# One encoder layer in fp32: the sum into v ahead of late weight rows, pair 0's scores first, decayed keys on ScalarE, output-weight sums on VectorE, one gate ahead of one normalisation

## The chip, the core and the metric

The kernel runs on one core of a Trainium2 chip. The metric is the device time of one execution in microseconds (us), and a time is the median of several runs.

The engines are called as the profile calls them. PE is TensorE (PEld its weight loads), DVE is VectorE, ACT is ScalarE, POOL is GpSimd. SP is SyncE, which only issues transfers (its queue is SPq).

## The reference

The program computes one encoder layer for two sequences of 1024 tokens with 1024 channels. Cut to what matters here:

```
h = rmsnorm(x) * (1 + scale1) + shift1                  # scale, shift, gate: silu(c) @ w_ada + b_ada
q, k, v, g_sw, p, gate_a, gate_b = split(h @ w_in)      # 8 heads, dk = 64, dv = 128
q, k = rope(q), rope(k) / 8
per chunk of 128 tokens, forward and backward:
    inner = ((q_c @ k_c.T) * decay_in) @ v_c
    cross = (q_c * decay_q) @ state
    state = decay_chunk * state + (k_c * decay_k).T @ v_c
ret      = forward + backward, normalised per head
branch_a = silu(g_sw) * ret * gain
branch_b = (pooled(p) @ w_pool) * pool_scale
merged   = sigmoid(gate_a) * branch_a + sigmoid(gate_b) * branch_b
x = x + gate1 * (merged @ w_out)
x = x + gate2 * mlp(modulated rmsnorm(x))               # up, 3-tap convolution, gelu * linear, down
y = rmsnorm(x)
```

## The kernel before

**Precision and products.** Every large product is made of passes over a high and a low fp32r part of the operands. ACT copies a raw weight piece to its high part, POOL subtracts to get the low part. Products of 2 x 2 blocks are done with 7 block products instead of 8. For that, sums of weight quarters are needed (POOL makes most of them) and sums of results (DVE adds a PSUM bank into a tile that ACT has copied).

**Stages.** For each sequence: the mixer in four head pairs (`pr` 0 to 3, two heads each), the output product (`out`), the norm of the middle, the MLP. This change touches the mixer's four pairs and what the output product reads.

**Order.** Each engine runs its own list, written out by hand, and waits on counting semaphores. Nothing is reordered at run time, so an instruction that waits holds up all that stands behind it on its engine, and this is as true of SP's list of transfers.

**One pair on PE.** In pairs 1 to 3: seven qkv products (o = 0 to 6, `qkv_products`, L1457). The last of them, o = 6, adds into a bank whose other half must first have been added to v, so it waits for `q_summed` 2, which DVE's `qkv_add(1)` (L2810, v_sb) gives. Then `pool_unit` (L1476) with the turning of q and k between its halves, the scores (L1555), and 21 unit products (L1525), written (s, o) with s = 0 to 2 and o = 0 to 6. Behind certain of these stand the small products: `products(h)`, keys times values (KV0, KV1; L1544), which waits for DVE's `scores(h)` (L2879) and for the decayed keys (`kd_done`); `outputs(h)` (O0, O1; L1569); `turn_ret(h)` (TR0, TR1; L1310), which waits for DVE's `normed(h)` (L2910); and `branch_b(h)` (BB0, BB1; L1579). Unit product (1, 6) waits for DVE's `unit_add(1, 1)` (L2819, bufA). Pair 0 makes q, k and v in another way (`first_qkv`) and has the scores behind (0, 3), KV0 behind (0, 4).

**DVE in a pair.** Besides these it makes four levels of the pooling (`pool_level`, L2985), the recurrent states (L2866), the statistics, the swish and the gates. All of it is one list per pair, printed below.

**Late rows.** 32 tiles of 128 x 1024 of w_ada per sequence (`late_tile`, L2647) are reduced on DVE in spots 0 to 5 of each pair, two in a spot, as `LATE_AT` says: none ahead of spot 4 of pair 0, none after spot 1 of pair 3. They sit in a ring of two buffers. SP loads one (L773) when the tile two before it has been reduced, at a fixed place among the other loads.

**Sums of output weights.** For the output product of both sequences, four units u of w_out (each 128 x 4 x 512, 1 MB) are loaded into `out_unit` (L890), summed in place by four subtractions or additions, and stored to DRAM (`out_sums`, L895). There is one buffer, so load u + 1 waits for store u, which waits for sums u. Its memory is that of the late rows' ring, so load 0 waits for the last late tile. All this lies in sequence 0, pair 3, and before this change the sums run on POOL, between weight pieces.

## Time and profile before

| | |
|---|---|
| median of 3 runs | 2626.63 us (2625.64 to 2629.75) |
| the profiled execution's own time | 2632.94 us |
| its span, first to last instruction | 2631.1 us |
| mean granted clock of PE | 0.984 |
| busy: PE, DVE, POOL, ACT | 2536.4, 1866.0, 1732.4, 1145.4 us |

The span is read from the first instruction to the last; the execution's own time is 1.8 us longer. The profiled execution lies 6.3 us above the median of the runs. Sequence 0's mixer pairs take 96 to 600 us of the span, sequence 1's 1394 to 1888 us. In a timeline row the first number is the start, the second the time that the merged instructions take together, and the bracket behind it says how long the engine had stood still before them and who released it.

### The profile page before, as it was taken

The numbers are of one execution on the slowest core, as the hardware profiler recorded it, in microseconds if no ns is written. First come the engines' busy times: TensorE is split into PE (matmuls) and PEld (weight loads), VectorE is DVE, ScalarE is ACT, GpSimd is POOL, SyncE is SP. The second block draws the span as 40 slices with busy tenths as digits, with TensorE's granted clock in tenths as the row PEclk, the third lists the DMA queues.
The fourth block names the chain that finished last, engine by engine and source line by source line (L and its number), as shares of the span: only waits on it lengthen the run. The fifth ranks groups of instructions, "written<-read, shape, count | busy, mean of one in ns | idle before, by whom it ended". The sixth has DMA issues, their size and how long they took to land.

```text
span 2631.1 us, 34797 instructions
## 1 busy us (share of the span) xinstructions
PE 2536.4 (96%) x12684; PEld 2121.1 (81%) x12684; DVE 1866.0 (71%) x2246; ACT 1145.4 (44%) x1738; POOL 1732.4 (66%) x1181
## 2 busy tenths in 40 slices
PE   6899999989999999999998999999999999999998
PEld 3788888868778888878887888888877888888886
DVE  4978898866786666665868888888778645556434
ACT  5332323225555454555623323232456545454443
POOL 1675767786287777645656858586564877775545
PEclk9999999999999999999999999999999999999998
DMA  8124242346144455497631423332440333325764
GB/s 325 40 83 133 82 133 83 110 175 221 48 147 138 160 172 169 153 322 249 190 114 41 131 84 110 105 111 73 167 149 25 112 112 112 110 80 185 213 194 145
DMA packets 296010, 362.15 MB, mean 138 GB/s; under 512 B 17313, under 2 KB 178465, under 8 KB 295841
## 3 DMA queue, kind: packets, MB, share of 16 engines
q1 hardware_dynamic: 292960, 349.44, 41.2%
q10 hardware_dynamic: 2880, 10.49, 1.1%
q8 instruction: 103, 1.69, 0.3%
q14 instruction: 67, 0.54, 0.1%
HBM read 284.36 MB, written 75.50 MB: 137 GB/s over the span
## 4 chain that ended last, share of the span: by engine, by line
PE 65%; DVE 15%; POOL 7%; issue 6%; DMA 4%; ACT 3%; SPq 1%; DVEq 0%; POOLq 0%; ACTq 0%
PE ps L1095 26%; PE ps L1261 14%; PE ps L1525 7%; PE ps L1156 4%; PE ps L1476 3%; POOL f_w L2162 3%; PE ps L1366 2%; PE ps L1457 2%; DVE late_rows L2647 2%; PE ps L1193 2%; DMA late_rows<-in_w_late 2%; PE ps L1544 1%; DVE merged_t L2962 1%; POOL grs L2183 1%; DVE bufB L2924 1%
## 5 line engine op out<-in xcount | busy, mean ns | idle before, releaser
L2223 POOL TENSOR_TENSOR f_w<-f_ring,f_w 128x512 fp32r<-128x512 f32 x434 | 596.1, 1379 | 399.3 <-ACT f_w L1812 394.0
L1095 PE MATMUL ps<-hc_hi,f_w 128*128 128x512 f32 x2240 | 690.5, 389 | 3.5 <-ACT u_act L1886 2.8
L2162 POOL TENSOR_TENSOR f_w<-f_ring,f_w 128x512 fp32r<-128x512 f32 x282 | 443.7, 1585 | 301.8 <-ACT f_w L1646 301.7
L1095 PEld LDWEIGHTS ps<-hc_hi,f_w 128*128 128x128 f32 x2240 | 419.9, 188 | 93.1 <-ACT u_act L1886 3.6
L1095 PE MATMUL ps<-hc_lo,f_w 128*128 128x512 f32 x1120 | 435.8, 389 | 0.0
L1261 PE MATMUL ps<-act_ring,f_w 128*128 128x512 f32 x1848 | 421.7, 390 | 3.8 <-DVE act_ring L2542 2.9
L1261 PEld LDWEIGHTS ps<-act_ring,f_w 128*128 128x128 f32 x1848 | 346.5, 188 | 77.9 <-issue 4.9
L1812 ACT ACTIVATE f_w<-f_ring 128x512 fp32r<-128x512 f32 x434 | 269.8, 624 | 256.3 <-POOL f_ring L2233 109.5
L1525 PE MATMUL ps<-hb,f_w 128*128 128x512 f32 x1440 | 349.2, 397 | 2.7 <-POOL f_w L2162 2.2
L1646 ACT ACTIVATE f_w<-f_ring 128x512 fp32r<-128x512 f32 x282 | 175.4, 627 | 369.6 <-POOL f_ring L2170 140.2
L1525 PEld LDWEIGHTS ps<-hb,f_w 128*128 128x128 f32 x1440 | 268.8, 189 | 65.4 <-issue 9.6
L2542 DVE TENSOR_TENSOR act_ring<-f_ring,act_ring 128x512 fp32r<-128x512 f32 x154 | 149.8, 978 | 173.2 <-ACT act_ring L1864 172.8
L1095 PEld LDWEIGHTS ps<-hc_lo,f_w 128*128 128x128 f32 x1120 | 210.2, 188 | 43.7
L1457 PE MATMUL ps<-f_w,hb 128*128 128x256 f32 x1440 | 174.7, 283 | 0.0
L1457 PEld LDWEIGHTS ps<-f_w,hb 128*128 128x128 f32 x1440 | 174.0, 192 | 0.5
L1864 ACT ACTIVATE act_ring<-f_ring 128x512 fp32r<-128x512 f32 x154 | 97.0, 630 | 162.7 <-PE ps L1261 147.7
L1156 PE MATMUL ps<-out_ring,f_w 128*128 128x512 f32 x672 | 154.7, 391 | 0.2 <-DVE xT L2563 0.2
L1525 PE MATMUL ps<-ht,f_w 128*128 128x512 f32 x576 | 144.2, 400 | 8.0 <-ACT gate_rows L1682 7.3
L1156 PEld LDWEIGHTS ps<-out_ring,f_w 128*128 128x128 f32 x672 | 125.9, 188 | 27.6 <-issue 1.0
L1525 PEld LDWEIGHTS ps<-ht,f_w 128*128 128x128 f32 x576 | 107.0, 190 | 32.8 <-ACT gate_rows L1682 8.9
L2647 DVE SCALAR_TENSOR_TENSOR late_rows<-late_rows,silu_row 128x1024 f32<-128x1024 f32 x64 | 108.9, 1736 | 26.5 <-DMA late_rows<-in_w_late 26.5
L2249 POOL TENSOR_TENSOR f_w<-f_ring,f_w 128x512 fp32r<-128x512 f32 x56 | 82.7, 1484 | 50.5 <-ACT f_w L1829 50.1
(263 smaller groups left out, 4109.5 us busy)
## 6 DMA issues: line engine op xcount, KB each, us to landing
f_ring<-in_w_in SPq DMA_DIRECT2D x176, 256.0 KB, 4.9
f_ring<-in_w_up SPq DMA_DIRECT2D x160, 256.0 KB, 3.3
f_ring<-gated_out SPq DMA_DIRECT2D x154, 256.0 KB, 3.0
late_rows<-in_w_late SPq DMA_DIRECT2D x64, 512.0 KB, 3.7
gated_out<-gated_up SPq DMA_DIRECT2D x44, 512.0 KB, 4.2
f_ring<-down_sums SPq DMA_DIRECT2D x88, 256.0 KB, 3.0
gated_out<-t_gated SPq DMA_DIRECT2D x22, 768.0 KB, 6.5
f_ring<-in_w_down SPq DMA_DIRECT2D x66, 256.0 KB, 3.5
```

Of the source, the lines that this page charges most:

```text
L1095: ins = pe.matmul(ps_row[:, half_of(bank)], a[:, cols], b, start=i in (0, 1, 3) and k == 0 and n == 0, stop=k == KQ - 1 and n == 2, skip_g ...
L1156: ins = pe.matmul(ps_row[:, half_of(bank)], a[:, j * P:(j + 1) * P], b, start=i in (0, 1, 3) and c == 0 and o == 0, stop=c == PAIRS - 1 an ...
L1261: ins = pe.matmul(ps_row[:, half_of(bank)], a[:, j * P:(j + 1) * P], b, start=i in (0, 1, 3) and c == 0 and p == 0, stop=c == CHUNK_PAIRS ...
L1457: ins = pe.matmul(ps[:, Q_SLOT[i], t * 2 * P:(t + 1) * 2 * P], a[:, k, rows], b[:, cols], start=i in (0, 1, 3) and k == 0 and n == 0 and t ...
L1525: ins = pe.matmul(ps_row[:, half_of(bank)], a[:, cols], b, start=i in (0, 1, 3) and k == 0 and n == 0, stop=k == KQ - 1 and n == 2, skip_g ...
L1646: act.activation(mix_out(pr, q)[:, 0, :], mix_raw(mix_load(pr, q)), ACT.Copy).then_inc(mix_hi.sem, 1)
L1812: act.activation(piece_slot(q)[:, 0, :], piece_raw(q), ACT.Copy).then_inc(piece_hi.sem, 1)
L1864: act.activation(act_of(where[1], m)[0], ring_slot(UP_LOADS + 2 * m + 1), ACT.Copy).then_inc(a_hi.sem, 1)
L2162: pool.tensor_tensor(out[:, 1, :], raw, out[:, 0, :].bitcast(F32), ALU.subtract).then_inc(mix_lo.sem, 1)
L2223: pool.tensor_tensor(piece_slot(q)[:, 1, :], piece_raw(q), piece_slot(q)[:, 0, :].bitcast(F32), ALU.subtract).then_inc(piece_lo.sem, 1)
L2542: dve.tensor_tensor(low, ring_slot(UP_LOADS + 2 * m + 1), high.bitcast(F32), ALU.subtract).then_inc(a_lo.sem, 1)
L2647: dve.scalar_tensor_tensor(rows, rows, 0.5, silu_row[seq][:, :], ALU.mult, ALU.mult, accum_out=modT[:, seq, 16 + n:17 + n]).then_inc(late_ ...
```

## The change

Five things are moved. (1) In pairs 1 to 3, `qkv_add(1)`, the sum into v, comes ahead of the two late tiles of spot 1. SP issues the late loads of spot 5 two loads earlier. (2) In pair 0, DVE does the pooling levels and `scores(0)` ahead of `decayed_q(0)`, `unit_add(0, 2)` and `pool_means` behind the first states, and `swish(1)` right behind `swish(0)`; O1 stands behind (1, 5) instead of (1, 4). (3) `decayed_k(h)`, two multiplications of 128 x 8 x 64 for each head, goes from DVE to ACT, in every pair. (4) The four sums of each output unit go from POOL to DVE, at spots 2 to 5 of pair 3, and SP's loads and stores of the units are spread accordingly. (5) `gate_a(1)` comes ahead of `normed(1)`, in every pair.

```diff
-OUT_UNIT_AT = (("set", 0, 3), ("set", 1, 0), ("set", 1, 4), ("set", 2, 1))
+OUT_UNIT_AT = (2, 3, 4, 5)
...
-                    for j in range(KC - 2):
+                    for j in range(KC - 4):
                         mix_in(where, j)
                     late_loads(pr - 1, 5)
-                    for j in range(KC - 2, KC):
+                    for j in range(KC - 4, KC):
                         mix_in(where, j)
...
                     if with_units:
-                        for u in range(1, PAIRS - 1):
-                            out_unit_store(u)
-                            out_unit_load(u + 1)
+                        out_unit_store(1)
+                        out_unit_load(2)
...
                 for j in range(4):
                     out_ring_load(out, j)
+                if seq == 0:
+                    out_unit_store(2)
+                    out_unit_load(3)
                 sp.wait_ge(*filled(last_pair, "TR1"))
...
+            def decayed_k(where, h):
+
+                kdp, scale = mix_buffers[where[1]][2], T_DK + 2 * h
+                if h:
+                    act.wait_ge(*filled(where, "TK"))
+                else:
+                    act.wait_ge(*rope_done.at(where, 2 if where[2] else 4))
...
+                    ins = act.activation(dst, rot[:, :, P + h * DK:P + (h + 1) * DK], ACT.Copy,
+                                         scale=pairS[:, scale + d:scale + d + 1])
...
                     if pr:
                         copy_p(pair, 0)
+                        decayed_k(pair, 0)
                     piece_after(pair, p_piece(pr, 0))
                     if pr:
                         evac_k(pair)
+                        decayed_k(pair, 1)
                     else:
                         t_piece_high(pair, 3)
                     copy_p(pair, 1)
+                    if pr == 0:
+                        decayed_k(pair, 0)
...
+            def out_unit_sums(u):
+
+                a11, a12, a21, a22 = (out_unit[:, x, :] for x in range(4))
+                dve.wait_ge(unit_in, 32 * (u + 1))
...
                     def late(spot):
 
+                        if seq == 0 and pr == PAIRS - 1 and spot in OUT_UNIT_AT:
+                            out_unit_sums(OUT_UNIT_AT.index(spot))
...
                         late(0)
                         qkv_add(0)
                         rope_half(0)
+                        qkv_add(1)
                         late(1)
-                        qkv_add(1)
                         qkv_add(2)
...
+                    gate_a(1)
                     normed(1)
-                    gate_a(1)
```

DVE's list in sequence 0, pair 0, from the last low part of h (hb) to the second `scores`, before (rot is `scores(0)`, kdp from ps is `scores(1)`):

```order
L2760 TENSOR_TENSOR hb<-xT_49,hb 128x2048
L2833 TENSOR_SCALAR kdp_56<-rot,pairS 128x8x64 x2
L2985 SCALAR_TENSOR_TENSOR poolU<-p_in,pairS 128x1039
L3003 COPY qT_58<-ps 128x1024
L2833 TENSOR_SCALAR rot<-rot,pairS 128x8x64 x2
L2847 TENSOR_TENSOR qdT_59<-qT_58,dec 64x1024 x2
L2985 SCALAR_TENSOR_TENSOR poolU<-poolU,pairS 128x1037
L2985 SCALAR_TENSOR_TENSOR poolU<-poolU,pairS 128x1033
L2819 TENSOR_TENSOR swish_60<-swish_60,ps 128x512
L2879 SCALAR_TENSOR_TENSOR rot<-ps,dec 128x8x128
```

The same place in the changed kernel:

```order
L2785 TENSOR_TENSOR hb<-xT_49,hb 128x2048
L2993 SCALAR_TENSOR_TENSOR poolU<-p_in,pairS 128x1039
L3011 COPY qT_58<-ps 128x1024
L2993 SCALAR_TENSOR_TENSOR poolU<-poolU,pairS 128x1037
L2993 SCALAR_TENSOR_TENSOR poolU<-poolU,pairS 128x1033
L2993 SCALAR_TENSOR_TENSOR poolU<-poolU,pairS 128x1025
L2887 SCALAR_TENSOR_TENSOR rot<-ps,dec 128x8x128
L2844 TENSOR_TENSOR swish_60<-swish_60,ps 128x512
L2844 TENSOR_TENSOR bufB<-bufB,ps 128x512
L2855 TENSOR_TENSOR qdT_59<-qT_58,dec 64x1024 x2
L2887 SCALAR_TENSOR_TENSOR kdp_56<-ps,dec 128x1024
```

The decayed keys are gone from DVE, and `decayed_q` has gone from ahead of `scores(0)` to behind it.

DVE's list in a later pair, around the sum into v (v_sb), before:

```order
L2802 TENSOR_TENSOR rot<-bufA,bufB 128x16x32
L2647 SCALAR_TENSOR_TENSOR late_rows_0_74,modT<-late_rows_0_74,silu_row_72 128x1024
L2647 SCALAR_TENSOR_TENSOR late_rows_1_75,modT<-late_rows_1_75,silu_row_72 128x1024
L2810 TENSOR_TENSOR v_sb<-v_sb,ps 128x1024
L2810 TENSOR_TENSOR rot<-rot,ps 128x1024
```

And in the changed kernel:

```order
L2827 TENSOR_TENSOR rot<-bufA,bufB 128x16x32
L2835 TENSOR_TENSOR v_sb<-v_sb,ps 128x1024
L2670 SCALAR_TENSOR_TENSOR late_rows_0_74,modT<-late_rows_0_74,silu_row_72 128x1024
L2670 SCALAR_TENSOR_TENSOR late_rows_1_75,modT<-late_rows_1_75,silu_row_72 128x1024
L2835 TENSOR_TENSOR rot<-rot,ps 128x1024
```

The sum into v stands two late tiles earlier.

SP's list of transfers in sequence 0, pair 3, from load 0 of the units on, before (xT rows are x coming back, f_ring from w_out or merged_out are the first loads of the output product):

```order
L890 DMA out_unit<-in_w_out 128x2x512 x2
L802 DMA f_ring<-in_w_in 128x4x128 x4
L895 DMA out_sums<-out_unit 128x4x512
L890 DMA out_unit<-in_w_out 128x2x512 x2
L895 DMA out_sums<-out_unit 128x4x512
L890 DMA out_unit<-in_w_out 128x2x512 x2
L895 DMA out_sums<-out_unit 128x4x512
L890 DMA out_unit<-in_w_out 128x2x512 x2
L945 DMA xT_49<-in_xt 128x1024 x4
```

In the changed kernel:

```order
L890 DMA out_unit<-in_w_out 128x2x512 x2
L802 DMA f_ring<-in_w_in 128x4x128 x4
L895 DMA out_sums<-out_unit 128x4x512
L890 DMA out_unit<-in_w_out 128x2x512 x2
L945 DMA xT_49<-in_xt 128x1024 x4
L924 DMA f_ring<-in_w_out 128x512
L924 DMA f_ring<-merged_out 128x512
L924 DMA f_ring<-in_w_out 128x512
L924 DMA f_ring<-merged_out 128x512
L895 DMA out_sums<-out_unit 128x4x512
L890 DMA out_unit<-in_w_out 128x2x512 x2
```

The last piece starts at load 1 (load 0 and store 0 stand before it, with two f_ring loads between them). Load 3 now stands behind the four xT loads and the first four loads of the output product, where before all four unit loads stood ahead of them.

## Rows read from the trace of the kernel before

**Rows 1.** Part 1 of the page: busy time, share, instructions.

```profile
PE 2536.4 (96%) x12684; PEld 2121.1 (81%) x12684; DVE 1866.0 (71%) x2246; ACT 1145.4 (44%) x1738; POOL 1732.4 (66%) x1181
```

**Rows 2.** PE's waits over the whole span: total, times, longest, in us.

```profile
PE ps L1457 <- DVE v_sb L2810: 22.0, 6, 4.5
...
PE ps L1544 <- DVE rot L2879: 13.1, 2, 6.7
```

**Rows 3.** PE's waits in sequence 1's mixer alone, 1380 to 1890 us.

```profile
PE ps L1525 <- ACT gate_rows L1682: 2.3, 2, 1.7
```

**Rows 4.** PE's timeline: o = 5 of pair 1, first and last of six o = 6.

```profile
214.18 5.92 PE L1457 MATMUL ps<-f_w,hb 128*128 128x256 f32 x48
224.61 8.22 PE L1457 MATMUL ps<-f_w,ht 128*128 128x256 f32 x48 [4.51 <-DVE v_sb L2810]
...
1792.38 7.52 PE L1457 MATMUL ps<-f_w,ht 128*128 128x256 f32 x48 [2.79 <-DVE v_sb L2810]
```

**Rows 5.** Stretch of o = 6 in pair 1: length, PE busy, granted clock, DMA.

```profile
224.60:232.70 8.10, 8.09 (x49) 0.69 0.51 166
```

**Rows 6.** DVE's timeline around the sum into v, sequence 0, pair 1.

```profile
220.00 1.21 DVE L2647 SCALAR_TENSOR_TENSOR late_rows<-late_rows,silu_row 128x1024 f32<-128x1024 f32 x1
...
223.35 1.21 DVE L2810 TENSOR_TENSOR v_sb<-v_sb,ps 128x1024 f32<-128x1024 f32 x1
```

**Rows 7.** DVE's timeline at spot 5 of pair 0.

```profile
183.69 1.68 DVE L2647 SCALAR_TENSOR_TENSOR late_rows<-late_rows,silu_row 128x1024 f32<-128x1024 f32 x1 [4.62 <-DMA late_rows<-in_w_late]
```

**Rows 8.** PE's timeline in pair 0: KV0, KV1, and (1, 6).

```profile
120.60 3.58 PE L1544 MATMUL ps<-v_sb,kdp 128*128 128x128 f32 x16 [6.65 <-DVE rot L2879]
...
129.48 1.95 PE L1544 MATMUL ps<-v_sb,rot 128*128 128x128 f32 x16
...
156.37 2.89 PE L1525 MATMUL ps<-ht,f_w 128*128 128x512 f32 x12
```

**Rows 9.** DVE's timeline in pair 0: from decayed keys to unit_add(1, 1).

```profile
101.71 2.94 DVE L2833 TENSOR_SCALAR kdp<-rot,pairS 128x512 f32<-128x512 f32 x2
...
109.78 4.52 DVE L2847 TENSOR_TENSOR qdT<-qT,dec 64x1024 f32<-64x1024 f32 x2
114.33 4.40 DVE L2985 SCALAR_TENSOR_TENSOR poolU<-poolU,pairS 128x1037 f32<-128x1037 f32 x2
...
119.24 1.21 DVE L2879 SCALAR_TENSOR_TENSOR rot<-ps,dec 128x1024 f32<-128x1024 f32 x1
...
138.46 0.17 DVE L2854 MEMSET state<- 64x128 f32 x1 [2.74 <-PE ps L1570]
...
154.49 0.68 DVE L2819 TENSOR_TENSOR bufA<-bufA,ps 128x512 f32<-128x512 f32 x1
```

**Rows 10.** ACT's copies of 128 x 512, line L1682: ns min/median/max, starts.

```profile
L1682 ACT ACTIVATE swish<-ps x16: 596/597/598, 101.9 to 1824.8; 128x512 f32<-128x512 f32 x16
```

**Rows 11.** DVE's sums of the MLP's weight units, line L2536: ns min/median/max.

```profile
L2536 DVE TENSOR_TENSOR down_unit<-down_unit x44: 679/954/1783, 761.8 to 1152.3; 128x512 f32<-128x512 f32 x44
```

**Rows 12.** Loads of the output units, line L890.

```profile
DMA to landing us min/median/max: 3.7/4.8/5.5
```

**Rows 13.** Stores of the output units, line L895.

```profile
DMA to landing us min/median/max: 4.3/4.9/5.7
```

**Rows 14.** PE's timeline: o = 6 of pair 3 and start of out, both sequences.

```profile
492.53 7.48 PE L1457 MATMUL ps<-f_w,ht 128*128 128x256 f32 x48 [2.89 <-DVE v_sb L2810]
...
599.90 23.96 PE L1156 MATMUL ps<-out_ring,f_w 128*128 128x512 f32 x105
...
1877.02 1.03 PE L1310 MATMUL ps<-cst,tokb 128*128 128x128 f32 x8
...
1887.84 12.40 PE L1156 MATMUL ps<-out_ring,f_w 128*128 128x512 f32 x54
```

**Rows 15.** DVE's timeline, sequence 1, pair 3: `normed(0)` and the end of `branch_a(0)`.

```profile
1854.62 2.21 DVE L2910 TENSOR_TENSOR tokb<-tokb,grs 128x1024 f32<-128x1024 f32 x1
...
1866.74 1.27 DVE L2933 SCALAR_TENSOR_TENSOR swish<-ps,pairS,swish 128x1024 f32<-128x1024 f32 x1
```

More of the change, by code:

```diff
@@ L999, in _ @@
                     late_loads(pr, 2)
-                    for j in range(KC + 8, KC + 10):
-                        mix_in(where, j)
                     if with_units:
@@ L1004, in _ @@
                         out_unit_load(0)
+                    for j in range(KC + 8, KC + 10):
+                        mix_in(where, j)
                     late_loads(pr, 3)
-                    for j in range(KC + 10, MIX_LOADS):
-                        mix_in(where, j)
                     if with_units:
@@ L3040, in _ @@
                         states(0)
+                        unit_add(0, 2)
+                        pool_means()
                     else:
```

67 lines of the change are left out of this document (27 added, 40 removed).

## The prediction

> **What bounds the kernel now.** I read the busy times first. PE is busy 96% of the span, all others 71% or less [rows 1], so time can only be won where PE stands still or runs slowly, and every microsecond that it waits is one of the program, so long as PE is not merely made to wait at the next place. The second view is PE's waits. Outside the start, two groups stand out: six waits for the sum into v, 22.0 us, and two for `scores(0)` in pair 0, 13.1 us [rows 2]. A third, for ACT's copies in the gate sets, is 2.3 us in sequence 1's pair 0 [rows 3]; sequence 0's pair 0 is built alike, which makes 4.6. The third view is the timeline behind a wait. The 48 matmuls of o = 5 take 5.92 us, the same 48 of o = 6 behind the wait take 8.22 us in the first case and 7.52 in the last [rows 4]. In that stretch the granted clock is 0.69 of full: part of it runs at 1.2 GHz instead of 2.4 [rows 5]. So a wait of 2.8 us or more costs 1.6 to 2.3 us on top. The excess at the six places is between 6 x 1.6 and 6 x 2.3; most are near the low end, I take 10.8, which is their sum over the six rows. KV0 in pair 0 shows the same: 3.58 us against 1.95 for KV1 [rows 8], 1.6 more, twice.
>
> **The sum into v.** PE has finished o = 5 at 220.1 and waits until 224.6 [rows 4]. DVE meanwhile reduces two late tiles, from 220.0 to 223.4, and only then adds, 1.2 us [rows 6]. With the add first it ends at about 221.2 and 1.1 us of the 4.5 stay. A second edit takes these off too. DVE's work from spot 5 of the pair before to this sum has no slack, and it starts with a wait of 4.6 us for a late row whose load stood behind two weight loads [rows 7]. SP now issues it two loads earlier; a landing 3 us or more sooner puts the add ahead of PE's arrival. The tiles themselves don't vanish. Behind the add, DVE has 3.4 us of tiles, a 1.2 us add and then the rope, while PE has 5.9 us of o = 6 before it asks for `q_summed` 3: 4.6 (5.8 if both tiles take the slow 2.3 us) against 5.9 is just enough. The decayed keys, 2.9 us for the first head [rows 9], leave DVE in the same place, which gives the slack back before the scores. Term: 22.0 + 10.8 = 32.8, of which I leave 0.3, so 32.5. Its bounds are 24 (1.1 us stay at each place, with a little of the slow clock) and 34.
>
> **Pair 0.** DVE starts the first decayed key at 101.7 and `scores(0)` at 119.2; in between lie 4.5 us of `decayed_q(0)`, two pooling levels at 2.2 each and two pairs of decayed keys [rows 9]. Afterwards there are four levels, 8.8, and the copy of q, 1.2 (taken as the 1.21 of a 1024-wide operation that reads PSUM): `scores(0)` at 111.7, done at 112.9. PE gets to KV0 at 113.9 (120.60 less 6.65) and doesn't wait. The question is what is late next. It is `unit_add(1, 1)`, which (1, 6) waits for. Before, DVE took from 119.24 to 155.2 for it, 35.9 us. Off: two gaps in which DVE waited for PE, 2.7 each [rows 9] (the other is 2.7 too), and the last level, 1.5. On: `decayed_q(0)`, 4.5 (half of that if POOL is still), an add 0.6, and two waits for ACT's tanh, 1.2 each, since both swishes are now done ahead of the second states. That is 36.5, so it ends at 148.2 (146 to 150.5). PE, with 6.65 + 1.63 gone, would be at (1, 6) at 148.1 instead of 156.4 [rows 8], or about 1 us sooner with two small waits gone. So 8 us are won here and DVE's chain takes what is above that. Then `gate_a(1)` ahead of `normed(1)`: it ends the ACT wait of 1.7 us [rows 3], and puts one gate, 2.2 us, ahead of TR1. DVE waits for POOL's root at that point anyway, so the gate mostly fills a gap; I charge it 0.7: 1.0 net. Hence 9 a pair, 18 for both, less 1 for a slow stretch if the wait at (1, 6) should reach 3 us: 17. Bounds: 12 and 21.
>
> **Decayed keys on ACT.** Four activations a pair, 32 in all. The nearest row is ACT's copy of as many elements, 0.60 us [rows 10], so 2.4 us a pair; ACT is busy 44% [rows 1]. They stand behind waits that ACT had anyway (rope done, TK filled) and ahead of weight pieces made five products ahead of use. Cost on the path 0; if the cover were gone, the 1.2 us per head would show at the copy of k, at most 10 us in all over the pairs. ScalarE: Activation LUTs, section "What ACT_TABLE_LOAD costs", in the Trainium skill, gives an activation with a per-partition pointer operand as 280 ns + 0.833 ns an element, 0.71 us for 512; by it a pair is 2.8 us instead of 2.4, and no row here shows the form.
>
> **Pair 3 and the output units.** What handling them costs now is seen by comparing the sequences: from o = 6 of pair 3 to the first output product 107.4 us in sequence 0 and 95.5 in sequence 1, which has no units [rows 14]. 11.9 us is all that can be won. On DVE a sum of 128 x 512 in SBUF takes 0.68 to 1.78 us, median 0.95 [rows 11]; four make 3.8 us (2.7 to 7.1). The median is my value, as POOL works about as much here as in the MLP. Spot 2 falls where DVE waits for the turned q and costs nothing. The chain of one buffer is another matter. I use sequence 1's times. `normed(0)` ends at 1856.8 [rows 15]; sums(1) to 1860.6; store 4.9 [rows 13]; second half of the load issued 0.6 later and landed 4.8 after [rows 12]: 1870.9. DVE is past `branch_a(0)` at 1868.0 [rows 15], plus what the sums(1) have pushed it, and so waits for the load. Sums(2) to 1874.7, the bias part 0.6, the gate 2.2, `normed(1)` 2.2: 1879.7. TR1 was at 1877.02 [rows 14]: PE waits 2.7 us, with an even chance of 1.6 for the clock. Unit 3 comes the same way, load behind the xT loads and store 2, at spot 5, 1 to 2 us later than DVE is free; it delays the first output steps by about 1 us. Term: 11.9 - 2.7 - 0.8 - 1.4 = 7. Bounds: 11.9, and -3 with both sums at 7.1 and landings at 5.5.
>
> What this does to POOL argues for it as well: POOL's sums stood among the weight pieces. Against it speaks a rule of the Trainium skill (SBUF — State Buffer, "Who interferes with whom"): a VectorE operation with two SBUF inputs and a GpSimd operation that reads SBUF shut each other out for the whole instruction. By that rule each sum may wait for one POOL piece and the move only changes who waits; the rows' 0.68 to 1.78 for one form agree with it, and with every sum at the upper value the term would be 0 instead of 7.
>
> **Sum.** 32.5 + 17 + 7 = 56.5. The profiled execution took 2632.9 us in its own time and would take 2576.4; it lay 6.3 above the median, so the median goes from 2626.6 to 2570.
>
> **The rivals.**
> - *The unit chain is dearer than thought.* Waits at TR1 of 5 to 10 us and output steps held by `out_sums`: pair 3 gives 0 or -5. For it: one buffer, 10.3 us from sums to data, and SP's load 3 behind eight other transfers. Against it: only three such turns. Gain 45 to 49, time 2580.
> - *DVE stays the bound of the sum into v.* If the late row still lands late, or `unit_add(1, 1)` in pair 0 is 3 us later than I say, 8 to 16 us go. For it: the chain before v is without a gap, and landings vary. Time 2583.
> - *All of it is won*, PE waits for nobody: 32.8 + 21 + 11.9 = 66, time 2561. Against it: the chain of the units, which needs short sums and landings.
> - *Slower than before.* ACT's list is in order. If a decayed key waited there for something that comes late (its own `kd_done`, the turned k), every weight piece behind it would be late, and PE has a piece's work of 2.8 us in hand for each of five. It would have to cost more than 56 us, 7 us in each of 8 pairs. ACT's waits ahead of it are the ones it has now, so I see no place for it.
> - *No change.* It would need the won time to return at the end of each pair, as a DVE bound. DVE is busy 71% of the span [rows 1] and loses 5 us of keys a pair, so no.
>
> **Chances.** Forecast 0.60, units dearer 0.14, v or pair 0 still bound 0.12, all of it 0.08, slower 0.03, no change 0.03. To hold 8 in 10 the range goes from the full gain, 2558, over both dearer cases to 2592; the likeliest case alone is 2563 to 2578. A measurement of this kernel tells about 0.2% (5 us) from no change. Faster 0.94, within 0.2% 0.03, slower 0.03.
>
> **What the new profile would show.** Right: no wait of PE on v_sb over 1.5 us and o = 6 at 5.9 us in all six pairs; KV0 in pair 0 without a wait; DVE idle for 1 to 4 us on `out_unit` at spot 4, and a PE wait at TR1 of sequence 0's pair 3; ACT's decayed keys at 0.6 to 0.7 us. Wrong: PE waiting for f_w behind ACT; waits on bufA at (1, 6) of several us; late rows still awaited at spot 5; ACT or DVE waiting on f_ring loads in the output product.

## The result, and the profile after

| | before | after |
|---|---|---|
| median of 4 runs | 2626.89 us (2625.64 to 2629.75) | 2592.85 us (2591.01 to 2594.57) |
| ratio, 95% interval | | 0.9869 (0.9852 to 0.9886) |
| profiled execution, own time / span | 2632.94 / 2631.1 us | 2591.01 / 2588.9 us |

The change makes the kernel 34 us faster. 56.5 were forecast, and the time is 1 us above the range. The profiled executions lie 42 us apart, 8 more than the medians: the one of before is 6.3 above its median, the one of after 1.8 below. Some 3 of these 8 us can be named. In the execution of before a stretch at the start of sequence 1 (1353.3 to 1360.5 us) ran at a granted clock of 0.57 with no wait of PE ahead of it: 18 matmuls took 7.2 us, which at the rate of the 78 of the same line behind them (17.84 us) take 4.1. In the changed kernel's execution they take 4.4.

One run of `a1_load_back` below took 3143.94 us at a granted clock of 0.751, one run of before 14216.26 and one 5017.46; the ratios leave these three out, the medians do not (that of `a1_load_back` would be 2577.4).

PE's waits in the changed kernel (total, times, longest, in us; compare [rows 2]):

```profile
PE ps L1527 <- DVE bufA L2844: 7.0, 7, 2.5
PE ps L1459 <- DVE v_sb L2835: 6.6, 6, 1.1
PE ps L1312 <- DVE rot L2827: 5.0, 6, 0.9
...
PE ps L1158 <- DVE out_ring L2572: 4.8, 1, 4.8
```

Line numbers have moved: L1459 are the qkv products (L1457 before), L1527 the unit products (L1525), L1312 the turns (L1310), L1158 the output product (L1156), L2835 `qkv_add`, L2844 `unit_add`, L2887 `scores`, L2670 `late_tile`. The waits of 22.0 us for v and 13.1 for the scores [rows 2] are down to 6.6 and 0. But v is still awaited at all six places, where I had expected next to nothing; PE waits at six places for q and k behind the rope (`rot`), which it did not before; and it waits at (1, 6) and at the first output product. The timeline of PE shows the same, in pair 1 (against [rows 4]), in pair 0 (against [rows 8]) and at the end of sequence 0's pair 3 (against [rows 14]):

```profile
113.61 1.95 PE L1546 MATMUL ps<-v_sb,kdp 128*128 128x128 f32 x16
...
148.97 3.02 PE L1527 MATMUL ps<-ht,f_w 128*128 128x512 f32 x12 [1.97 <-DVE bufA L2844]
...
213.29 6.02 PE L1459 MATMUL ps<-f_w,ht 128*128 128x256 f32 x48 [1.13 <-DVE v_sb L2835]
...
225.58 1.97 PE L1312 MATMUL ps<-cst,rot 128*128 128x128 f32 x16 [0.81 <-DVE rot L2827]
...
547.29 4.39 PE L1527 MATMUL ps<-ht,f_w 128*128 128x512 f32 x12 [2.46 <-DVE bufA L2844]
```

KV0 comes without a wait; o = 6 takes 6.02 us, without the slow clock.

**What holds DVE now.** DVE's own waits ahead of v, first before, then after:

```profile
DVE late_rows L2647 <- DMA late_rows<-in_w_late: 26.5, 6, 5.3
...
DVE gate_rows L2942 <- ACT gate_rows L1692: 7.2, 6, 1.2
```

```profile
DVE gate_rows L2950 <- ACT gate_rows L1694: 29.9, 6, 6.2
...
DVE late_rows L2670 <- DMA late_rows<-in_w_late: 1.7, 2, 0.9
```

The wait for the late row is nearly gone, 24.8 us of it, and 22.7 us have come back as a wait for ACT's tanh, which `branch_b` multiplies. The timelines of DVE, POOL and ACT at the end of pair 0 show from where (three fences, in this order):

```profile
170.65 1.23 DVE L2670 SCALAR_TENSOR_TENSOR late_rows<-late_rows,silu_row 128x1024 f32<-128x1024 f32 x1 [0.76 <-DMA late_rows<-in_w_late]
...
180.01 1.22 DVE L2950 SCALAR_TENSOR_TENSOR gate_rows<-gate_rows,ps 128x1024 f32<-128x1024 f32 x1 [6.17 <-ACT gate_rows L1694]
```

```profile
172.82 1.54 POOL L2195 TENSOR_TENSOR f_ring<-f_ring 128x512 f32<-128x512 f32 x1 [4.09 <-DMA f_ring<-in_w_in]
```

```profile
174.46 0.63 ACT L1648 ACTIVATE f_w<-f_ring 128x512 fp32r<-128x512 f32 x1 [8.27 <-POOL f_ring L2195]
178.32 0.63 ACT L1648 ACTIVATE f_w<-f_ring 128x512 fp32r<-128x512 f32 x1 [3.23 <-POOL f_ring L2195]
178.86 1.04 ACT L1694 ACTIVATE gate_rows<-gate_rows 128x1024 f32<-128x1024 f32 x1
```

Read backwards: DVE waits for the tanh at 178.86. ACT had its input since 173.8 (DVE's add into `gate_rows` ends there), but a weight piece of the next pair stands right ahead of it in ACT's list, another ahead of that, and these wait for POOL's sums. POOL's first sum adds load 4 of the next pair (L2195, `loads[2]`), and waits 4.1 us for it. Load 4 is one of the two that the change put behind 1 MB of late rows on SP's queue.

### The profile page after: what moved, and what is told of

Read it like the earlier page. It is cut to its first block, busy times and chain, and to the rows that moved or that the text cites. A ratio compares the mean times of both kernels' runs of the same rounds, so it can differ in the third digit from the quotient of the medians.

```text
span 2588.9 us, 34797 instructions
## 1 busy us (share of the span) xinstructions
PE 2518.4 (97%) x12684; PEld 2104.9 (81%) x12684; DVE 1859.0 (72%) x2230; ACT 1166.0 (45%) x1770; POOL 1722.0 (67%) x1165
## 4 chain that ended last, share of the span: by engine, by line
PE 66%; DVE 15%; POOL 8%; issue 5%; DMA 4%; ACT 3%; SPq 1%; POOLq 0%; DVEq 0%; ACTq 0%
PE ps L1097 27%; PE ps L1263 14%; PE ps L1527 8%; PE ps L1158 5%; POOL f_w L2187 4%; PE ps L1368 3%; PE ps L1478 2%; DVE late_rows L2670 2%; DMA f_ring<-in_w_in 1%; PE ps L1195 1%; POOL f_ring L2195 1%; DVE merged_t L2970 1%; PE ps L1546 1%; DVE bufB L2820 1%; POOL grs L2208 1%
## 5 line engine op out<-in xcount | busy, mean ns | idle before, releaser
L1527 PE MATMUL ps<-hb,f_w 128*128 128x512 f32 x1440 | 347.4, 395 | 0.0
L1527 PEld LDWEIGHTS ps<-hb,f_w 128*128 128x128 f32 x1440 | 268.3, 188 | 61.3 <-issue 6.7
L1459 PE MATMUL ps<-f_w,hb 128*128 128x256 f32 x1440 | 175.4, 283 | 2.1 <-ACT v_sb L1665 1.1
L1459 PEld LDWEIGHTS ps<-f_w,hb 128*128 128x128 f32 x1440 | 174.2, 192 | 3.1 <-issue 1.4
L1158 PE MATMUL ps<-out_ring,f_w 128*128 128x512 f32 x672 | 156.9, 395 | 4.8 <-DVE out_ring L2572 4.8
L1158 PEld LDWEIGHTS ps<-out_ring,f_w 128*128 128x128 f32 x672 | 127.4, 190 | 33.0 <-ACT f_w L1849 5.2
L1527 PE MATMUL ps<-ht,f_w 128*128 128x512 f32 x576 | 144.1, 399 | 7.0 <-DVE bufA L2844 7.0
L1527 PEld LDWEIGHTS ps<-ht,f_w 128*128 128x128 f32 x576 | 107.0, 190 | 30.8 <-DVE bufA L2844 8.6
L2670 DVE SCALAR_TENSOR_TENSOR late_rows<-late_rows,silu_row 128x1024 f32<-128x1024 f32 x64 | 115.7, 1841 | 1.9 <-DMA late_rows<-in_w_late 1.7
```

Source lines behind the costliest of these rows:

```text
L1158: ins = pe.matmul(ps_row[:, half_of(bank)], a[:, j * P:(j + 1) * P], b, start=i in (0, 1, 3) and c == 0 and o == 0, stop=c == PAIRS - 1 an ...
L1459: ins = pe.matmul(ps[:, Q_SLOT[i], t * 2 * P:(t + 1) * 2 * P], a[:, k, rows], b[:, cols], start=i in (0, 1, 3) and k == 0 and n == 0 and t ...
L1527: ins = pe.matmul(ps_row[:, half_of(bank)], a[:, cols], b, start=i in (0, 1, 3) and k == 0 and n == 0, stop=k == KQ - 1 and n == 2, skip_g ...
L2670: dve.scalar_tensor_tensor(rows, rows, 0.5, silu_row[seq][:, :], ALU.mult, ALU.mult, accum_out=modT[:, seq, 16 + n:17 + n]).then_inc(late_ ...
```

## The experiments

Each kernel is compared with the kernel before by runs on the same chip at the same time; the ratio carries the comparison, since the medians of before move by 2 us from group to group (2626.9 to 2629.2). An interval is about 0.13% to either side, 3.4 us, so two kernels of different groups closer than some 5 us are not told apart. Differences from the base below are differences of medians; for the parts of the change the value by the ratios stands beside them. "The base" is the changed kernel with the late load put back, the first experiment.

| label | what | median us | ratio, 95% interval |
|---|---|---|---|
| a1_load_back | the base | 2578.07 | 0.9812 (0.9799 to 0.9825) |
| a2_v_only | before + v ahead of late tiles | 2602.10 | 0.9904 (0.9891 to 0.9917) |
| a3_v_load | the same + early late load | 2605.02 | 0.9920 (0.9907 to 0.9933) |
| a4_tanh_first | changed kernel, tanh ahead of a piece | 2577.33 | 0.9813 (0.9801 to 0.9825) |
| d4_load_mid | changed kernel, late load one load later | 2577.91 | 0.9814 (0.9798 to 0.9829) |
| c1_units_pool2 | base, unit sums on POOL | 2575.91 | 0.9798 (0.9783 to 0.9813) |
| c2_keys_dve2 | base, keys on DVE | 2590.67 | 0.9857 (0.9841 to 0.9874) |
| c3_pair0_back2 | base, old order in pair 0 | 2577.76 | 0.9806 (0.9791 to 0.9820) |
| c4_gate_back2 | base, gate behind normalisation | 2586.81 | 0.9841 (0.9827 to 0.9856) |
| d1_add_first | base, unit_add(1, 1) early, all pairs | 2596.17 | 0.9881 (0.9866 to 0.9896) |
| d2_sums_last | d1 + last unit's sums later | 2601.39 | 0.9898 (0.9885 to 0.9912) |
| d3_pool_add_first | c1 + unit_add(1, 1) early | 2591.01 | 0.9860 (0.9844 to 0.9875) |
| e1_pair0_chain | base, pair 0: add early, silu late | 2583.38 | 0.9831 (0.9817 to 0.9845) |
| e2_units_order | base, units ahead of xT on SP, sums(1) later | 2579.29 | 0.9814 (0.9801 to 0.9826) |
| e3_both | e1 + e2 | 2588.47 | 0.9847 (0.9835 to 0.9860) |
| e4_both_mid | e3, late load one load earlier | 2588.63 | 0.9847 (0.9834 to 0.9860) |
| f1_tiny_sums | base, sums of 8 of 512 columns | 2573.72 | 0.9787 (0.9774 to 0.9800) |
| f2_xt_last | base, xT behind eight output loads | 2578.47 | 0.9805 (0.9791 to 0.9818) |

### The late load

```diff
 a1_load_back, against the changed kernel
-                    for j in range(KC - 4):
+                    for j in range(KC - 2):
                         mix_in(where, j)
                     late_loads(pr - 1, 5)
-                    for j in range(KC - 4, KC):
+                    for j in range(KC - 2, KC):
 a4_tanh_first, against the changed kernel (pairs 0 to 2)
+                        early = pr < PAIRS - 1 and (s, o) == (2, 5)
+                        if early:
+                            tanh_gate(pair, 2, 0)
                         piece_after(pair, set_piece(pr, s, o))
```

`a2_v_only` swaps `late(1)` and `qkv_add(1)` in the kernel before, `a3_v_load` does this and has KC - 4, `d4_load_mid` has KC - 3 in the changed kernel.

> The changed kernel with one edit undone: the load of the late rows of spot 5 stands again behind two more weight loads. Theory A (the prediction's: the late row was what held DVE's chain ahead of v): DVE waits 4 to 5 us for the row again at each of the six places, the wait for the sum into v goes from 1.1 to 3 us or more at each, o = 6 takes 7.5 us again, 15 to 25 us in all: 2608 to 2618. Theory B (the early late load only moved the wait: it pushes two weight loads back, POOL's first sum of the next pair waits 4.1 us for one of them, ACT's piece stands behind that, and its tanh for branch_b behind the piece, which is the 6.2 us for which DVE now waits): the wait for tanh falls from 29.9 us in six to about 10, the wait for the late row comes back with about 20, and the time stays within 5 us of 2593.

> The kernel before with the sum into v ahead of the two late tiles of spot 1, and nothing else. By the prediction's working (2.3 to 3.4 us of tiles off each wait, 1.1 us stays, little of the slow clock stays) 24 us are won: 2603. The rival counts also the new wait at the turn of q and k, which the changed kernel shows with 0.8 us at each of six places: then 19 us are won, 2608, with six waits of PE on rot.

> The kernel before with the whole first part (the sum into v ahead of the tiles, and the late load of spot 5 two loads earlier), and nothing else. Theory A: the load is worth 8 us beside the order alone, since the wait of 1.1 us at v and the slow clock go: 8 us below the run with the order alone, about 2595. Theory B: the load gives what it takes, within 3 us of the run with the order alone, and DVE waits 25 to 30 us for ACT's tanh instead of 26 us for the late rows.

> The changed kernel with ACT's tanh of the second gate's first half ahead of one weight piece of the next pair (pairs 0 to 2). Theory B: DVE's wait for tanh falls from 6 us to about 2 at each place, the chain ahead of v starts 4 us earlier, and PE's waits on v (6.6 us in six) and at the turn of q and k (5.0 in six) go: 11 us, 2582. Rival: the weight piece that is made 1 us later is itself awaited (PE waited 1.0 us for f_w at the first qkv product of pair 1): then f_w waits of 1 us or more appear at the first qkv products and half of it is lost, 2588. Theory A sees no gain, since the tanh is not what holds DVE: 2593.

> The changed kernel with the late load of spot 5 one weight load ahead of where it was before instead of two (loads 5, 6 and 7 behind it). Theory B in its exact form: POOL's first sum of the next pair adds load 4, which in the changed kernel takes 5.3 us to land behind 1 MB of late rows, against 3.0 us ahead of them. With load 4 ahead again POOL's first sum is on time, its second one, with load 5, about on time; DVE's waits for tanh and for the late row are both 1 to 3 us a place, and the time is the base's, 2575 to 2580. If it was something else in the order, such as load 5, it stays near 2590.

Putting the load back is worth 15 us. Theory A, the prediction's, is out. Theory B had the place and missed the size: it kept the time within 5 us of 2593. DVE and POOL in the base, at the same place:

```profile
173.91 1.93 DVE L2670 SCALAR_TENSOR_TENSOR late_rows<-late_rows,silu_row 128x1024 f32<-128x1024 f32 x1 [4.95 <-DMA late_rows<-in_w_late]
...
179.88 1.22 DVE L2950 SCALAR_TENSOR_TENSOR gate_rows<-gate_rows,ps 128x1024 f32<-128x1024 f32 x1 [1.20 <-ACT gate_rows L1694]
```

```profile
169.63 1.29 POOL L2195 TENSOR_TENSOR f_ring<-f_ring 128x512 f32<-128x512 f32 x1 [1.80 <-DMA f_ring<-in_w_in]
```

Here the row is late again and the tanh on time, and at this place `branch_b` starts at the same moment. At the other places it gains: the six waits for the row are 16.3 us, the six for tanh 7.2, together 8 less than the 31.6 of the changed kernel, and PE waits for v at one place of six (1.6 us) and at one turn (0.3). PE's waits in the qkv products and at the turns of q and k are 13.7 us in the changed kernel and 1.9 in the base, 11.8 apart; the two profiled executions lie 12.1 apart. Loads 4 and 5 were issued nearly at the same time in both kernels (167.5 and 166.6 us). What differs is how long they took. Their landing times in the changed kernel (with two more loads; loads 4 and 5 alone took 5.2 to 5.5), then in the base:

```profile
DMA to landing us min/median/max: 5.2/5.6/5.7
```

```profile
DMA to landing us min/median/max: 2.9/3.0/3.2
```

So the late rows did not so much delay the issue of the loads behind them as their landing. `a4` leaves the loads as they are and only takes the tanh out from behind the piece, and wins the same 15 us; DVE's wait for the first tanh falls from 29.9 to 9.4 us, though POOL's wait for the load stays (28.0 us in six):

```profile
DVE gate_rows L2953 <- ACT gate_rows L1694: 9.4, 6, 2.3
```

```profile
POOL f_ring L2198 <- DMA f_ring<-in_w_in: 28.0, 6, 5.4
```

`d4` moves load 4 alone ahead again, and wins it too. So the chain (load 4, sum, piece, tanh, `branch_b`) is cut at two links, at the load by `a1` and `d4` and at the tanh by `a4`, and each cut gives the same time: the chain is shown. The links between them, POOL's sum and ACT's piece, are read from the timelines. It matters less in the kernel before: `a3` is 3 us behind `a2`, which is inside the intervals, and the gain of 8 us that theory A gave the early load did not come there either. There v has 1.1 us of wait at two places, and at four with the early load.

`a2` alone is worth 24.8 us (25.2 by the ratio): the sum into v ahead of the tiles gives nearly all that this part gives. The wait at the turn that the rival counted follows from it in part: 1.7 us at two places, and 3.6 at four with the early load.

### The other parts, each taken back

`c1` puts `out_unit_sums` and SP's order of before back, `c2` the `decayed_k` of DVE, `c3` DVE's and PE's order of pair 0 without the keys, and `c4` is two lines:

```diff
-                    gate_a(1)
                     normed(1)
+                    gate_a(1)
```

> Base for this and the next three: the changed kernel with the late load put back (2578.1). Here the sums of the output units go back to POOL, with the loads and stores of before. The prediction's working has their move to DVE worth 7 us, so 2585, with the out product again starting 107 us behind v. Rival (the chain of one buffer is dearer): the changed kernel's trace shows 3.2 us won up to the first output product, of which 1.6 are lost again in the output steps, so 2580, and PE's wait of 4.8 us on out_ring becomes waits for f_w of about the same size.

> The base with the decayed keys back on DVE, in pair 0 ahead of the first level and behind the copy of q as before. The keys' move alone was priced at 0, as part of pair 0's and v's terms. Theory C: the keys count only in pair 0, where 5.8 us stand ahead of the first scores again: KV0 waits about 4 us twice, with 1.6 of slow clock, 2589. Theory D: in the later pairs too DVE has no slack from the rope to the scores, so the second head's states and then (1, 6) come later in all eight pairs: 2600 or more. If ACT paid for the keys somewhere, the time falls instead.

> The base with pair 0's order of before, the keys staying on ACT. Without 5.8 us of keys the old order has the first scores at about 113.4 instead of 119.2: KV0 waits 1 to 2 us instead of 6.7. If the order was what won pair 0's 17 us, this run is at 2590 or more; if the keys were, it is within 5 us of the base, 2578 to 2583. My value 2583, with the wait of ACT's copies (1.7 us) back in part.

> The base with the second normalisation ahead of the gate again. The prediction charged this edit with 0.7 us for a gain of 1.7 in a pair: ACT's copy into the gate rows waits for the gate again and PE for ACT, 1.0 net in each pair, 2586 if it holds in all eight pairs and 2580 if only in the two pairs 0. Rival: the root that DVE waits for is ready by now, nothing changes, 2578.

**c2, c3.** Without the keys on ACT the time rises by 12.6 us (11.8 by the ratios), as theory C had it. PE waits 7.5 us at KV0 in two places, and the 28 matmuls behind each of these waits take 1.8 us more than in the changed kernel's pair 0. PE in `c2`, sequence 0's pair 0:

```profile
117.36 3.05 PE L1546 MATMUL ps<-v_sb,kdp 128*128 128x128 f32 x16 [3.83 <-DVE rot L2899]
120.07 3.67 PE L1527 MATMUL ps<-hb,f_w 128*128 128x512 f32 x12
```

Once the keys have moved, the order of pair 0 is worth nothing. With the old order back, PE waits 2.1 us for the scores in each pair 0, and no longer 2.0 at (1, 6): one wait is exchanged for the other. With the keys on DVE the new order still shortens KV0's wait, from 6.65 us [rows 8] to the 3.83 above, so its 0 is the price behind the keys' move and not the price by itself, which no run here gives.

**c4.** The gate ahead of the normalisation is worth 8.7 us (7.6 by the ratios), four times what I gave it. PE in `c4`, sequence 1's pair 0:

```profile
1420.57 3.02 PE L1527 MATMUL ps<-ht,f_w 128*128 128x512 f32 x12 [1.97 <-DVE bufA L2844]
1440.64 4.60 PE L1527 MATMUL ps<-ht,f_w 128*128 128x512 f32 x12 [2.63 <-ACT gate_rows L1684]
```

The wait for ACT's copy is back with 2.6 us in each pair 0, 1.6 of slow clock behind one, and 0.7 in pair 3; and because DVE reaches the end of the pair later, v and the rope are awaited at three places each (5.8 us together, against 1.9 in the base).

**c1.** The units' move is worth nothing, if not less. With the sums back on POOL, from o = 6 of pair 3 to the first output product it is 102.4 us (471.02 to 573.42) against 101.6 in the base (470.02 to 571.63), and up to the first matmuls of the middle norm 0.3 us less than in the base. PE's waits are others, not fewer: 3.0 us at the turns back and 1.6 for f_w, instead of 2.5 at (1, 6) and 4.8 at the first output product. `c1` is the fastest kernel with the whole computation, but its interval overlaps with the base's (2.2 us less by the medians, 3.7 by the ratios).

### Attempts at what is left

The base's PE still waits 7.0 us on bufA and 4.8 on out_ring.

```diff
 d1_add_first, against the base
                     unit_add(1, 0)
+                    unit_add(1, 1)
                     centred(0, None)
                     normed(0)
                     late(3)
-                    unit_add(1, 1)
```

`e1_pair0_chain` does this in pair 0 alone, and puts `silu_of_rows` behind `branch_a(0)`.

> The base (the changed kernel with the late load put back, 2578.1) with unit_add(1, 1), for which PE waits at (1, 6), ahead of the centring and normalisation of the first head in every pair. In the base PE waits 2.0 us there in each pair 0 and 2.5 in sequence 0's pair 3, 7.0 in all with some small ones. If nothing else is late in its place, all of it goes: 2571.5. Rival: the normalised first head, 0.7 us later, is then late for its turn behind (1, 6), or pair 3's wait reappears at TR1, and only the two pairs 0 are won: 2574.

> The base (late load put back, 2578.1), in pair 0 alone with unit_add(1, 1) ahead of the first head's centring and the silu of the conditioning row behind branch_a(0). Theory: DVE's chain up to branch_a(0) bounds pair 0 (in the base it ends 0.3 us before PE reaches BB0, so taking the wait at (1, 6) away alone only moves it there, as the run with the add first in every pair showed with 1.8 us at BB0). The silu, 1.7 us, off this chain lets 1.7 to 2.0 us go in each pair 0: 2574.5. Rival: the bound is the add alone and both waits of 2.0 us go, 2574, which the trace tells apart by the wait at BB0; or DVE is late again at the second head's normalisation, and nothing is won, 2578.

`d1` is 18 us slower than the base, against all that I expected. The reason is in DVE's timeline, pair 1:

```profile
277.01 0.69 DVE L2844 TENSOR_TENSOR bufA<-bufA,ps 128x512 f32<-128x512 f32 x1 [4.85 <-PE ps L1527]
```

In the later pairs PE makes (1, 4), whose bank `unit_add(1, 1)` adds, behind O1, and in pair 0 ahead of it. DVE now stood 4.85 us for it with the normalisation queued behind, and then was late for everything: PE waited 9.9 us at seven turns and 13.1 at seven `branch_b`. I had looked at who waits for the add, not for whom the add waits. In pair 0, where it does not wait, the wait of 2.0 at (1, 6) came out 1.8 us long at BB0. `e1` cut into that chain, and the wait at BB0 fell to 0.9; but the silu reads the memory of the first late row, whose load now went out late, DVE waited 4.1 us for it and PE 3.5 at the second turn in each pair 0:

```profile
161.69 2.19 DVE L2670 SCALAR_TENSOR_TENSOR late_rows<-late_rows,silu_row 128x1024 f32<-128x1024 f32 x1 [4.14 <-DMA late_rows<-in_w_late]
```

`d3` did to `c1` what `d1` did to the base, with much the same loss, 15 us against 18.

> Unit sums on POOL as before, the late load put back (the run of that kind gave 2575.9), and unit_add(1, 1) ahead of the first head's normalisation. There PE waits 4.6 us on bufA, 2.0 in each pair 0, and 3.0 at the turns of pair 3. The waits on bufA go: 2572. If the sums on DVE are worth anything once their waits are gone, the two runs above are below this one.

For the units, `d2` has the last unit's sums behind the first two low parts, `e2` store 2 and load 3 ahead of the xT loads and sums(1) behind `unit_add(1, 1)`, `f2` all five xT loads behind the output product's first eight, and `f1` shrinks the sums (`out_unit[:, x, 0:8]`).

> The run before it, and in sequence 0's pair 3 the sums of the last output unit behind the first two low parts of the output product, with its store behind six more loads. In the base DVE stands 5.3 to 5.9 us at spot 5 for load 3 and PE 4.8 us at the first output product for it. If the wait for load 3 is the cause, PE's wait goes: 2567. Rival: the branch_b and merge of the pair, now 3 to 5 us later, hold the output steps instead, and the time is the same as without the edit.

> The base, in sequence 0's pair 3 with the sums of unit 1 behind unit_add(1, 1), and on SP's queue store 2 and load 3 of the units ahead of the four xT loads. In the changed kernel store 2 took 8.5 us to land with these and four other loads around it, the other three 4.3 to 4.7, and load 3, which DVE waits for 5.3 us and PE behind it 4.8, goes out only then. Theory: without them store 2 lands in 5 us, PE's wait at the first output product falls to about 1 us, and the wait of 2.5 us at (1, 6) moves to BB0: 2574. Rival: the weight loads for the output product are then late and PE waits for f_w or out_ring there instead, 2578.

> The base with the sums of the output units cut to 8 of 512 columns (the other columns of the sums are left out, so the output of the layer is not the reference's; all loads, stores and waits stay). It takes 11 us of DVE's time in pair 3 away and leaves the transfers. Theory T (the transfers bound the end of pair 3: 3 to 4 MB at 350 to 400 GB/s, with ACT's second piece of the output product waiting 11 us for its load): PE's wait at the first output product stays at 4 to 5 us, only the 2.5 us at (1, 6) go, 2576. Theory S (the sums on DVE are what eats the 7 us): both go, 2571 or less.

> The base with the five xT loads at the end of sequence 0 and 1's pair 3 behind the output product's first eight loads instead of ahead of them and of load 3. Theory T: store 2 lands in under 5 us instead of 8.0, load 3 and the output product's loads 4 to 7 go out 3 us sooner and have the DMA for themselves, PE's wait of 4.8 us falls to 0 to 2: 2574. Rival: the loads behind these, or the xT for the first update, are late instead and PE waits inside the output product: 2578 or more.

`d2` took nothing off: it is 5 us behind `d1`, and PE waits 9.9 us in three places for the output product's operands instead of 6.4 in one.

`f1` takes 9.0 us of DVE's time for the sums away (17.1 in the base, 8.1 now, by the groups of line L2554 to L2559; the expectation's 11 was too much) and wins 4.4 us (6.6 by the ratios): the 2.5 at (1, 6), and 1.3 at the first output product. There PE still waits 3.6 us. ACT says why, in the base:

```profile
568.85 0.63 ACT L1849 ACTIVATE f_w<-f_ring 128x512 fp32r<-128x512 f32 x1 [11.11 <-DMA f_ring<-in_w_out]
```

It waits 11 us for a load of the output product, and 10.9 in `f1`. SP issues this load after load 3, load 3 after store 2 has landed, and the slowest store takes 8.0 us in the base, 8.5 in the changed kernel and 9.1 in `f1`, with medians of 4.4 to 5.1; that it is store 2 is seen from load 3, which goes out 8.1, 8.5 and 9.1 us behind it. Windows of the changed kernel from the time sums(2) are made and while store 2 is out (length, PE, PEld, DVE, ACT, POOL busy, granted clock, DMA share, GB/s):

```profile
557.00:560.00 3.00, 3.00 (x11) 1.83 (x10) 2.79 (x6) 0.00 (x0) 0.00 (x0) 1.00 1.02 410
560.00:568.40 8.40, 8.40 (x42) 6.86 (x41) 4.89 (x6) 2.76 (x5) 3.82 (x3) 1.00 0.80 285
```

In stretches of two microseconds the DMA share is 0.96 to 1.05 from 554 to 566 us, and 0.27 in the last 2.4 us of the second window: the DMA engines are full until store 2 is nearly out. Hence taking the xT loads out of the way only moves the lack. In `e2` store 2 lands in 4.3 us, and ACT waits 14.4 us for the output product's load, behind the xT, so PE waits 7.6 us. In `f2` PE starts the output product with a wait of 1.1 us, at 569.41, 2.2 us sooner than the base, and waits 3.4 us and more inside it:

```profile
569.41 22.06 PE L1156 MATMUL ps<-out_ring,f_w 128*128 128x512 f32 x96 [1.07 <-DVE out_ring L2570]
594.90 1.70 PE L1156 MATMUL ps<-out_ring,f_w 128*128 128x512 f32 x6 [3.44 <-DVE out_ring L2570]
```

Four orders of the same transfers (base, `e2`, `f2`, `c1`) give the same time within the intervals. Of PE's 7.3 us in pair 3 of the base (2.5 at (1, 6), 4.8 at the first output product) 3.7 went with the sums and 3.6 stayed with the transfers. `f1`'s 2573.7 lies halfway between what theories T and S gave, so T is right for the larger part of the last wait, and not for all that pair 3 loses.

> The two before it together. If pair 0's chain and the units' chain are separate, the gains add up: 2570. If one of them is not real, this run shows the other alone, 2574.

> The run before it with the late load of spot 5 one weight load earlier, the setting that gave 2577.9 against 2578.1 with the load put back. It takes 1 to 3 us off DVE's waits ahead of v, where PE still waits 1.6 us in one place of six: 2568 if that counts, 2570 if not.

`e3` and `e4` carry the loss of `e1`, and 5 us more. In `e3` PE waits 10.9 us at three turns back (6.9 at two in `e1`), 6.5 at the first output product (4.0) and 3.4 at `branch_b` (1.8), for 2.2 less at (1, 6); why the one turn takes 5.4 us where `e1` has 3.5 was not looked for. They show no gain to add.

## Why the prediction was wrong

**The sum into v (32.5 forecast).** The order alone gives 24.8, and my lower bound for it was 24. The step that failed is the second edit's: "a landing 3 us or more sooner puts the add ahead of PE's arrival". The row did land some 4 us sooner for DVE (its wait fell from 4.6 to 0.8 in pair 0). I priced what that gains and took SP's two overtaken loads for free. POOL's sum, ACT's piece and the tanh stood behind load 4. The edit costs 15 us in this kernel, so that about 10 are left of the 32.5. Two waits of DVE changed places, the late row's and the tanh's, and over the six places its waits ahead of v fell only from 33.7 us to 31.6: at 212.0 the add began 1.1 us later than PE needed it.

A second step failed beside it, by less. "4.6 against 5.9 is just enough" holds for what it compares: the add that gives `q_summed` 3 ended at 218.6, and PE was done with o = 6 at 219.3. But the rope itself stood in the sum without a time. From 218.7 to 225.5 it took DVE 6.8 us where PE has 5.6 us of products ahead of the turn, and PE waited 0.8 us there at each of six places. Before the change the same four operations took 3.7 us (225.7 to 229.4). POOL was busy for 5.5 of the 6.8 us and for 0.2 of the 3.7, so the stretch before shows the rope with POOL still.

**Pair 0 (17).** The times were right within 1 us: the scores at 110.85 (forecast 111.7), `unit_add(1, 1)` done at 148.9 (148.2), no wait at KV0. The wait at (1, 6) is 2.0, since DVE was 0.7 later than forecast and PE came at 147.0, 1.1 ahead of the 148.1. But the term laid the gain on the order, and did not split it. The 0 of the keys' own paragraph is their cost on the path, and it holds; their gain is 12.6, and the order's behind them 0. The gate, which stood with 2 net, is worth 8.7. The term came out at 21 by the medians and 18 by the ratios, partly by luck: some of the gate's gain lies in pair 3 and at later sums into v. For the gate I had counted two pairs, and missed pair 3 (ACT waits of 3.3 us in sequence 0's before) and the shorter chain to the next pair's v.

**Decayed keys on ACT.** They take 0.71 to 0.73 us each (706 to 727 ns in all 32), not the 0.60 of the copy. The estimate from the figure of the Trainium skill, ScalarE: Activation LUTs, "What ACT_TABLE_LOAD costs", was 0.71, so rule and trace agree. Nothing on PE's path waits for them.

```profile
L1725 ACT ACTIVATE kdp<-rot,pairS x16: 706/710/719, 99.1 to 1764.9; 128x512 f32<-128x512 f32 x16
```

**The output units (7).** Measured about 0, the range was -3 to 11.9. The failed step is the 11.9: "all that can be won" was the difference of the two sequences before, but 2.75 us of it were a wait for ACT's gate copies and 1.4 the slow clock behind it, which the gate's edit took. The rest I gave to POOL's time, and much of it belongs to the transfers: with sums of 8 columns on DVE PE still waits 3.6 us. With the sums on POOL it is split between POOL's list and its wait for a unit (6.8 us in `c1`), and no run takes these apart. (The sum also takes off 1.4 for a delay that the text before it calls about 1 us.) My row for a store, 4.9 [rows 13], was right for three of four; the fourth shares the DMA engines with four xT and four output loads and takes 8.5, for which the prediction had no term. DVE's idle time at spot 4 (3.3 us) is as forecast, at spot 5 (5.3) three times as long; the wait forecast at TR1 (2.7) did not come, and one of 2.5 came at (1, 6), behind sums(1), which I had let cost nothing ahead of it. Sums(1) took 1.67 to 1.78 us each, 6.9 in all where I had 3.8, sums(2) and (3) 0.69. The windows of both show POOL busy for 6.58 of 6.80 us in the one and for none in the other:

```profile
539.80:546.60 6.80, 5.03 (x27) 4.04 (x25) 6.73 (x6) 1.90 (x3) 6.58 (x5) 1.00 0.00 0
```

By the rule of the Trainium skill that I had weighed (SBUF — State Buffer, "Who interferes with whom"), this is what two inputs in SBUF cost beside POOL; the trace agrees with it, at 1.0 us a sum. `f1` shows it purer. A sum of 8 columns takes 0.17 us when POOL is still, and beside POOL as long as a POOL piece (1.3 us) lets it wait:

```profile
534.07 1.25 DVE L2554 TENSOR_TENSOR out_unit<-out_unit 128x8 f32<-128x8 f32 x1
...
564.01 0.17 DVE L2554 TENSOR_TENSOR out_unit<-out_unit 128x8 f32<-128x8 f32 x1 [5.17 <-DMA out_unit<-in_w_out]
```

Of the 1.7 to 1.8 us of a sum beside POOL about 1.0 is a wait for POOL's instruction, and shrinking the sum does not shrink that wait.

**Sum.** The base takes 48.8 us off, 43.6 of them by its parts one by one (24.8, 12.6, 8.7, and -0.3 and -2.2 for the order of pair 0 and the units). By the ratios it is 49.4, and the parts are 25.2, 11.8, 7.6, -1.6 and -3.7, 39.3 in all. The first part was added to the kernel before and the others taken from the base, and each has an uncertainty of some 5 us, so the remainder of 5 to 10 us is not given a cause here. Take off the 15 that the late load costs, and the 34 are there. Of the 23 us between forecast and result, 8 are the two profiled executions' distances from their medians: I worked with one execution, and carried its 6.3 us over as an offset as if it were fixed.

Of the signs listed for the new profile, KV0, the keys, DVE's idle time on `out_unit` and o = 6 held (6.0 us at all six places); "no wait on v over 1.5 us" held and told me too little, since six waits of 1.1 us and six new ones of 0.8 passed under it. The PE wait at TR1 did not come, and of the signs of being wrong the waits on bufA at (1, 6) came, 2.0 us in each pair 0 and 2.5 in pair 3. Two rivals were right in part. "The unit chain is dearer than thought" gave pair 3 a gain of 0 or -5, which is what it has, and named load 3 behind eight other transfers, though not the waits that came; the 7 us that I gave this part are missing. "DVE stays the bound of the sum into v" had the place of the larger loss, but it looked for a late row and not for what the row's load pushes back.

## What to carry to other kernels

When a load is moved ahead of others, follow each overtaken load to its first reader and on through the in-order lists behind that; here it went through POOL and ACT back to the very engine that was to be relieved. Before an instruction is moved forward in an in-order list, look at what it waits for itself, in every stage that shares the code, and at whose memory it uses. A wait of an engine is worth only what is left once the next one of the same chain is reached, so take parts back one at a time: behind the keys' move the order of pair 0, which looked like the heart of the change, was worth nothing, and two lines at its edge 8 to 9 us.

## What the runs showed of the hardware

- The landing time of a load depends on what is in the queues around it: two 256 KB loads took 3.0 us ahead of two late rows and 5.3 behind them, a 1 MB store 4.3 with little beside it and 8.5 among eight loads, where one stretch shows 410 GB/s. The Trainium skill, DMA: Bandwidth & Descriptors, "Issuing engines are not separate DMA queues", says that transfers run on the same 16 DMA engines and interleave, whichever engine started them. All transfers of these stretches are started by SP, so the traces agree with the interleaving, and the part on different issuing engines no run here shows.
- The same wait of PE, 2.46 us at (1, 6) of pair 3, was followed by 12 matmuls of 3.01 us in the base and of 4.39 and 4.60 us in the changed kernel and in `e1` (granted clock 1.00, 0.65 and 0.62). So the length of a wait alone does not say whether PE comes back at 2.4 GHz or partly at 1.2.
- A slow stretch also came with no wait of PE ahead of it (1353.3 us in the profile of before, clock 0.57), and made that execution 3 us longer. The 3.9 us ahead of it are 32 matmuls of one column each. At the same place the 18 matmuls behind these 32 take 6.4 us in the base (clock 0.65) and 4.4 in the changed kernel (1.00), so two profiled executions can differ by 3 us at a place that the change does not touch.
